# Single-pass masks and forget sums, and pages of values laid over 64 partitions, in a two-group decoder step

## The chip, the cores and the metric

The kernel runs on one core of one Trainium2 chip. The metric is the device time of one execution in microseconds (us); lower is better. Before the change three runs took 2627.09, 2624.44 and 2619.4 us, median 2624.44.

## The reference

One layer of a hybrid decoder trunk is computed for a prompt of 512 tokens and for a sample group of 8 sequences with 4 new tokens each, on the same weights (model width 2048, all in float32). A normalised input is projected into four mixers of 512 channels: causal pooling, a gated linear recurrence, forgetting attention (8 heads of 64) and stick-breaking attention (8 heads of 64). Their outputs are normalised by group, projected back and added; then a squared-ReLU MLP of width 8192 is added. The change touches only the two attentions:

```
# forgetting attention: c_all is the running sum of the log forget gates
s = q.k * 64**-0.5 + cq - ck_t;  s = where(kpos <= qpos, s, -inf)
p = softmax(s);  y = p @ v
# stick-breaking attention, strictly causal
z = q.k * 64**-0.5;  log_1m = where(kpos < qpos, log_sigmoid(-z), 0)
w = where(kpos < qpos, exp(log_sigmoid(z) + reverse_cumsum(log_1m) - log_1m), 0);  y = w @ v
```

The sample group attends to 2048 past tokens per sequence. They lie in 16 pages of 128 tokens, found through a page table; the keys of a page are 256 KB and its values are 256 KB, for each of the two attentions.

## The kernel before, in words

The kernel has three stages, closed off by `end_stage`. Stage 1 is the input projection with the pooling, the recurrence and the head norms. Stage 2 is both attentions. Stage 3 is the output projection and the MLP. In stages 1 and 3 TensorE multiplies in the type float32r: weights and activations are split into a high and a low part, `w_hi` and `w_lo`, and the products at L419 and L424 run on those.

Stage 2 is written out by hand as a loop of 32 units (`UNITS`, L1808 on TensorE, L1483 on VectorE). A unit i is one prompt head and one block of 128 queries, i = 4h + q, and it does that block for the forgetting head (x = 0) and the stick-breaking head (x = 1) together; its scores have n = 128(q+1) columns, so 128, 256, 384 and 512 in turn. Beside every two units one sample step u (0 to 15) runs: u = 2b + x is sequence b, attention x. So an even u (fox) runs beside units of 128 and 256 columns, an odd u (sb) beside 384 and 512. "Block" below means this period of one u and two units.

What a block does on TensorE, in order: `seq_scores(u)` (the queries against 2048 past keys, L1745, after all four `k_loaded` semaphores), `seq_combine(u-1)`, then for each unit a part of the early output projection (`early_product`, L1803), `scores(i)`, the transposes of the unit before (`turn`, L1703), and its product with the values (`weigh`, L1718). At the end of the second unit comes `seq_weigh(u)` (L1782): the transposed probabilities against the past values, four steps c = 0 to 3, each after its semaphore `v_loaded[c]` and each with 4 column strips j.

`scores(i)` (L1677) makes three kinds of product into PSUM: the forget sum (L1684: a one-hot column of the identity, repeated over 128 columns, picks the head's row of `c_prompt`, 8 rows by n columns), the query-key products (L1689), and one 128-column product per attention with the identity that adds the causal mask (L1692). All are float32. Ahead of L1689 TensorE waits for `s_diff` of the unit before (VectorE, L1405).

Loads: SyncE loads the keys (`load_keys`, L610, 16 DMAs per u into `k_ring`, 128 partitions by 2048 bytes a page). It has one buffer and waits at L621 for `d_score`, the end of `seq_scores(u)`, before it issues the keys of u+1; behind those keys on its queue come the stores of partial sums, the next early weights and the next residual halves. GpSimd loads the values (`load_values`, L812): 16 DMAs per u, page 4j + c into `v_ring` slot c, strip j, 128 partitions by 2048 bytes, one token per partition. It waits at L820 for `d_av`, so slot c is refilled when step c of the `seq_weigh` before is done. The sample probabilities `d_p` (128 rows by 512 keys, and 32 new ones) are transposed in four 128-column pieces in `seq_turn` (L1754).

At the start of stage 2 VectorE makes `c_prompt` with one scan (L1360), GpSimd clears the padded queries `q_pad` (L808), ScalarE stores ten transposed value tiles (`v_store`, L968), and TensorE waits for all of them and for the constants `dconst` (L1669 to L1675) before block 0.

Of the kernel before, what the change touches and what calls it, by code (L numbers as in the profile page):

```python
# [24 lines left out]
P = 128  # L25
# [16 lines left out]
ROWS = 32  # L42
# [18 lines left out]
V_SLOTS, X_SLOTS = 4, 6  # L61
# [5 lines left out]
for _name, _n in _W:  # L67
# [5 lines left out]
_K = [("ident", P), ("ones", P), ("same_head", P), ("fox_mask", P), ("sb_mask", P),  # L73
      ("pool_rec", GT * POOL_MAX), ("before", P), ("minus_one", 1)]
# [16 lines left out]
def build_step(nc, xT, weights, w_early, params, consts, dconsts, pool_w, lru_w, state_pool,  # L91
# [38 lines left out]
    decay = r.take("decay", [P, 2, PAGE * 4 + NEW])  # L130
    r = Region(A_RAW, A_PROJ)
# [49 lines left out]
    c_prompt = r.take("c_prompt", [HEADS, SEQ])  # L181
    xh = [r.take(f"xh{i}", [P, HALF]) for i in range(X_SLOTS)]
    r = Region(A_ACT, A_END)
    v_ring = r.take("v_ring", [P, V_SLOTS, 4, D_GROUP])
# [121 lines left out]
    new_lf = sem("new_lf")  # L306
    c_ready = sem("c_ready")
# [39 lines left out]
    v_loaded = [sem(f"v_loaded{c}") for c in range(4)]  # L347
# [396 lines left out]
    def _(pool):  # L744
# [61 lines left out]

        for x in range(2):
            own.then(nc.gpsimd.memset(q_pad[x][:], 0.0))  # L808
# [23 lines left out]
    def _(act):  # L832
# [89 lines left out]
        for c in range(C_OUT):  # L922
            g, step = lru_step(c)
            if c + 1 < C_OUT:
                high_part(act, c + 1)
            if c == 0:
                input_squares()
            if c == 1:
                softplus_lam()
            if c == 2:  # L930
                forget_log()
            if step == 1:
# [43 lines left out]
        for n in range(10):  # L976
            v_store(n)
        act.wait_ge(kv_stored, 16 * 3)
# [154 lines left out]
    def _(dve):  # L1133
# [179 lines left out]
        for c in range(C_OUT):  # L1313
# [38 lines left out]
            if c >= 1:  # L1352
# [7 lines left out]
        v.tensor_tensor_scan(c_prompt[:], ones[0:HEADS, 0:1].to_broadcast([HEADS, SEQ]), logit[:, 0:SEQ], 0.0,  # L1360
                             ALU.mult, ALU.subtract).then_inc(c_ready, 1)
# [3 lines left out]
        for x in range(2):  # L1365
# [6 lines left out]
            v.tensor_copy(k_new[x][:], proj[:, (FK, SK)[x], :, SEQ:]).then_inc(q_padded, 1)  # L1372

# [216 lines left out]
    def _(pe):  # L1590
# [78 lines left out]
        pe.wait_ge(signs_in, 16)  # L1669
        pe.wait_ge(v_stored, 10)  # L1670
# [6 lines left out]
        def scores(i):  # L1677
# [6 lines left out]
            mm(s[0], ident[0:HEADS, h:h + 1].to_broadcast([HEADS, P]), c_prompt[:, 0:n], start=True, stop=False)  # L1684
# [64 lines left out]
        def seq_turn(u):  # L1749
# [3 lines left out]
            for c in range(4):  # L1753
                nc.tensor.transpose(bank[:, 5, P * c:P * c + P], d_p[:, P * c:P * c + P], ident)  # L1754
# [19 lines left out]
        def seq_weigh(u):  # L1774
            x = u % 2
            pe.wait_ge(d_ptsb, u + 1)
            for c in range(4):
                pe.wait_ge(v_loaded[c], 64 * (u + 1))
                if c == 3:
                    mm(bank[3 * ROWS:, 6], pt_new[:, 3 * ROWS:], v_new[x][:], start=False, stop=False)  # L1780
                for j in range(4):
                    ins = mm(bank[ROWS * j:ROWS * j + ROWS, 6], pt_t[:, c, ROWS * j:ROWS * j + ROWS], v_ring[:, (4 * u + c) % V_SLOTS, j],  # L1782
# [92 lines left out]
def constants():  # L1875
# [10 lines left out]
    put("fox_mask", np.where(j <= i, 0, MASKED).astype(np.float32))  # L1886
    put("sb_mask", np.where(j < i, 0, MASKED).astype(np.float32))
    _, g, t = np.indices((P, GT, POOL_MAX))
    put("pool_rec", (1.0 / np.minimum(2 ** (g + 1), t + 1)).astype(np.float32).reshape(P, -1))
    put("minus_one", np.full((P, 1), -1, np.float32))  # L1890
# [130 lines left out]
```

## Time and profile before

| | |
|---|---|
| three runs, us | 2627.09, 2624.44, 2619.4 (median 2624.44) |
| the profiled execution's own time, us | 2623.07 |
| its span, first to last instruction, us | 2621.4 |
| TensorE busy, us (share) | 2534.5 (97%) |
| weight loads / VectorE / ScalarE / GpSimd | 89% / 51% / 35% / 8% |
| mean granted TensorE clock | 0.989 of full |
| HBM read / written, MB | 340.20 / 13.74 |

All times in the trace are us from the start of the span, unless marked ns. PE is the TensorE matmul, PEld its weight load, DVE is VectorE, ACT ScalarE, POOL GpSimd, SP SyncE. One float32 product shows as two records, one float32r product as one. Lines such as L1745 are lines of the kernel. "DMA share" is the mean busy share of the core's 16 DMA engines; packets of different queues can overlap, so short windows go a little over 1.

### The profile page before, as it was taken

Reading aid. Unit: us, or ns where it says so; the run is one execution under the profiler, and the core shown is the slowest. Engines: PE = TensorE matmul, PEld = TensorE weight load, DVE = VectorE, ACT = ScalarE, POOL = GpSimd, SP = SyncE. Lnnn points to the kernel's source line nnn. Section 1 sums busy time; section 2 is a strip of 40 time slices with the busy share of each in tenths; the row PEclk is TensorE's granted clock in tenths of the full one; section 3 lists DMA queues with packets and bytes.
Section 4 is the critical chain, followed back from the end, with each engine's and each line's share of the span. In section 5 each row is a group of like instructions: output and inputs, shape, how many; then the busy total and the mean of one; then the engine's idle time right before and its main releaser. Section 6 shows DMA issues by size and latency. Waiting matters only on the chain.

```text
span 2621.4 us, 43516 instructions
## 1 busy us (share of the span) xinstructions
PE 2534.5 (97%) x16842; PEld 2331.3 (89%) x16842; DVE 1325.9 (51%) x1860; ACT 914.9 (35%) x1577; POOL 204.2 (8%) x320
## 2 busy tenths in 40 slices
PE   7999999999999979999999999999999999999998
PEld 7999998755565559999999999999999999999998
DVE  6345455334343456454554554554554554554555
ACT  5244455423232344332332332332332332332333
POOL 2060000133333300000000000000000000000000
PEclk9999999999999979999999999999999999999999
DMA  6293232699999932222222222222222222222222
GB/s 205 85 67 106 95 98 82 249 335 369 355 367 361 331 151 88 90 83 95 81 85 93 81 91 87 81 86 92 81 91 87 81 85 93 81 91 87 89 89 101
DMA packets 115362, 356.75 MB, mean 136 GB/s; under 512 B 30937, under 2 KB 39130, under 8 KB 90978
## 3 DMA queue, kind: packets, MB, share of 16 engines
q1 hardware_dynamic: 94402, 286.34, 33.1%
q0 software_dynamic: 20768, 67.65, 7.1%
q8 instruction: 145, 2.38, 0.4%
q14 instruction: 47, 0.39, 0.0%
HBM read 340.20 MB, written 13.74 MB: 135 GB/s over the span
## 4 chain that ended last, share of the span: by engine, by line
PE 85%; DVE 5%; issue 3%; ACT 3%; DMA 2%; SPq 2%; ACTq 0%; DVEq 0%
PE bank L419 48%; PE bank L424 24%; PE bank L1803 3%; PE bank L1745 2%; PE bank L1782 2%; DMA w_raw<-weights 1%; ACT w_hi L406 1%; DVE sum_tmp L488 1%; PE bank L1689 1%; PE bank L1684 1%; SPq L618 1%; SPq L622 1%; PE bank L1605 1%; ACT sum_tmp L482 1%; PE bank L1718 1%
## 5 line engine op out<-in xcount | busy, mean ns | idle before, releaser
L419 PE MATMUL bank<-x_act,w_hi 128*128 128x364 f32 (+1 forms) x4848 | 1061.9, 329 | 25.4 <-DVE x_act L500 13.1
L419 PEld LDWEIGHTS bank<-x_act,w_hi 128*128 128x128 f32 x4848 | 774.0, 189 | 28.0 <-issue 13.6
L419 PE MATMUL bank<-hid,w_hi 128*128 128x364 f32 (+1 forms) x3456 | 728.8, 329 | 18.6 <-DVE sum_tmp L488 17.6
L424 PE MATMUL bank<-x_act,w_lo 128*128 128x272 f32 x3232 | 650.5, 287 | 1.4 <-issue 1.4
L488 DVE TENSOR_TENSOR sum_tmp<-sum_tmp,bank 128x544 f32<-128x544 f32 x336 | 241.9, 720 | 723.2 <-ACT sum_tmp L482 723.2
L419 PEld LDWEIGHTS bank<-hid,w_hi 128*128 128x128 f32 x3456 | 555.0, 188 | 28.7 <-DVE sum_tmp L488 25.9
L424 PEld LDWEIGHTS bank<-x_act,w_lo 128*128 128x128 f32 x3232 | 563.1, 189 | 3.5 <-issue 2.2
L481 ACT ACTIVATE sum_tmp<-bank 128x184 f32<-128x184 f32 x336 | 108.7, 323 | 1021.9 <-PE bank L419 1021.8
L424 PE MATMUL bank<-hid,w_lo 128*128 128x272 f32 x2304 | 429.1, 287 | 0.0
L410 DVE TENSOR_TENSOR w_lo<-w_raw,w_hi 128x2048 fp32r<-128x2048 f32 x173 | 396.9, 2294 | 52.1 <-ACT w_hi L406 46.9
L424 PEld LDWEIGHTS bank<-hid,w_lo 128*128 128x128 f32 x2304 | 379.1, 188 | 0.0
L406 ACT ACTIVATE w_hi<-w_raw 128x2048 fp32r<-128x2048 f32 x173 | 331.4, 1916 | 8.8 <-DMA w_raw<-weights 8.8
L1524 DVE TENSOR_TENSOR x_res<-x_res,sum_tmp 128x544 f32<-128x544 f32 x272 | 196.8, 724 | 7.1
L482 ACT ACTIVATE sum_tmp<-bank 128x360 f32<-128x360 f32 x336 | 156.6, 466 | 0.0
L1803 PE MATMUL bank<-proj,wo 128*128 128x272 f32 x512 | 137.1, 399 | 3.3 <-DVE xh L1481 3.3
L488 DVE TENSOR_TENSOR proj<-proj,bank 128x544 f32<-128x544 f32 x36 | 25.9, 720 | 166.9 <-ACT proj L482 166.9
L1803 PEld LDWEIGHTS bank<-proj,wo 128*128 128x128 f32 x512 | 89.2, 190 | 20.1 <-issue 7.4
L821 POOL DMA_DIRECT2D v_ring<-sb_v x128 | 68.9, 538 | 142.7 <-issue 81.9
L821 POOL DMA_DIRECT2D v_ring<-fox_v x128 | 68.9, 539 | 135.8 <-issue 79.4
L481 ACT ACTIVATE proj<-bank 128x184 f32<-128x184 f32 x36 | 11.6, 323 | 173.9 <-PE bank L419 173.9
L1380 DVE TENSOR_REDUCE stat<-bank 128x1 f32<-128x128 f32 (+3 forms) x32 | 15.7, 492 | 110.8 <-PE bank L1692 110.8
L836 ACT ACTIVATE pa<-bank 128x128 f32<-128x128 f32 (+3 forms) x32 | 14.0, 438 | 150.8 <-PE bank L1692 150.8
(225 smaller groups left out, 1555.1 us busy)
## 6 DMA issues: line engine op xcount, KB each, us to landing
w_raw<-weights SPq DMA_DIRECT2D x173, 1024.0 KB, 4.8
k_ring<-fox_k SPq DMA_DIRECT2D x128, 256.0 KB, 5.1
v_ring<-fox_v POOLq DMA_DIRECT2D x128, 256.0 KB, 5.1
k_ring<-sb_k SPq DMA_DIRECT2D x128, 256.0 KB, 5.2
v_ring<-sb_v POOLq DMA_DIRECT2D x128, 256.0 KB, 5.4
wo<-w_early SPq DMA_DIRECT2D x16, 512.0 KB, 6.3
x_in<-xT SPq DMA_DIRECT2D x4, 1088.0 KB, 10.8
kv_out<-proj SPq DMA_DIRECT2D x4, 1088.0 KB, 9.8
```

What stands on the lines that cost most here:

```text
L406: nc.scalar.activation(w_hi[c0 % 2][:], w_raw[c0 % 2][:], ACT.Copy).then_inc(w_high, 1)
L410: nc.vector.tensor_tensor(w_lo[c0 % 2][:], w_raw[c0 % 2][:], w_hi[c0 % 2][:].bitcast(F32), ALU.subtract).then_inc(w_low, 1)
L419: ins = nc.tensor.matmul(bank[:, base + b, 0:n], hi, row[:, t:t + n], start=begin, stop=end)
L424: ins = nc.tensor.matmul(bank[:, base + b, 0:HALF], lo, row[:, t:t + HALF], start=False, stop=False)
L481: nc.scalar.activation(out[:, :, 0:EXTRA], bank[0:rows, b:b + 2, HALF:SPAN], ACT.Copy)
L482: nc.scalar.activation(out[:, :, EXTRA:], halves(bank[0:rows, b + 2, 0:2 * THIRD]), ACT.Copy).then_inc(extra, 1)
L488: nc.vector.tensor_tensor(out, out, bank[0:rows, b:b + 2, 0:HALF], ALU.add).then_inc(evac, 1)
L821: pool.dma_start(v_ring[:, n % V_SLOTS, j], (fox_v, sb_v)[x][bass.ds(page, 1)].rearrange("a p n -> (a p) n")).then_inc(v_loaded[c], 16)
L1524: v.tensor_tensor(x_res[:, t], x_res[:, t], sum_tmp[n % 2][:], ALU.add).then_inc(added, 1)
L1745: ins = mm(bank[ROWS * j:ROWS * j + ROWS, 4], q_pad[x][:, b, a], k_ring[:, j, :, a], start=(x == 1 and a == 0), stop=(a == 3))
L1782: ins = mm(bank[ROWS * j:ROWS * j + ROWS, 6], pt_t[:, c, ROWS * j:ROWS * j + ROWS], v_ring[:, (4 * u + c) % V_SLOTS, j], start=(c == 0), s ...
L1803: ins = mm(bank[:, 7, 0:HALF], wo[t % 2][:, k], y, start=(k == 0), stop=(k == 2 * GT - 1))
```

## The change

Four edits, all for stage 2:

- The masks: the two 128-column masks become one constant `diagonal` of 129 columns, and it and the identity are rounded copies of type float32r (three small ScalarE copies in stage 1, beside chunk 4). L1692 multiplies in float32r.
- The forget sums: the scan writes `pc`, ScalarE copies its float32r rounding into rows 0 to 7 of `c_prompt`, VectorE writes the rest into rows 64 to 71, GpSimd clears the tensor first, and L1684 becomes one float32r product over 72 rows with a constant that has a one in both rows of a head.
- The values: a page lies in 64 partitions of 4096 bytes (two tokens per partition); page c goes to partitions 0 to 63 for even c and 64 to 127 for odd c. There are two semaphores instead of four, and GpSimd waits once per two slots.
- The transposes at L1754 take every second column of two pages' 256 keys, so that rows and values match; the products at L1782 take `v_ring[:, c // 2, j, c % 2]`.

```diff
@@ load_values, GpSimd
-                n = 4 * u + c
+                m, o = c // 2, HEAD_DIM * (c % 2)
                 for j in range(4):
...
-                    if j == 0 and n >= V_SLOTS:
-                        pool.wait_ge(d_av, n - V_SLOTS + 1)
-                    pool.dma_start(v_ring[:, n % V_SLOTS, j],
-                                   (fox_v, sb_v)[x][bass.ds(page, 1)].rearrange("a p n -> (a p) n")
-                                   ).then_inc(v_loaded[c], 16)
+                    if j == 0 and c % 2 == 0 and u >= 1:
+                        pool.wait_ge(d_av, 4 * u - 2 + 2 * m)
+                    pool.dma_start(v_ring[o:o + HEAD_DIM, m, j].rearrange("p t n -> p (t n)"),
+                                   (fox_v, sb_v)[x][bass.ds(page, 1)].rearrange("a (p t) n -> (a p) (t n)", t=2)
+                                   ).then_inc(v_loaded[m], 16)
@@ GpSimd, start of stage 2
+        nc.gpsimd.memset(c_prompt[:].bitcast(F32), 0.0).then_inc(c_cleared, 1)
@@ ScalarE, stage 1, beside chunk 4
+                f(ident_r[:], ident, ACT.Copy)
+                f(diagonal_r[:], cc("diagonal", 0, P + 1), ACT.Copy)
+                f(two_rows_r[:], cc("two_rows", 0, HEADS), ACT.Copy).then_inc(const_round, 1)
@@ ScalarE, start of stage 2, after the fifth v_store
+                f(c_prompt[0:HEADS], pc[0:HEADS], ACT.Copy).then_inc(c_high, 1)
@@ VectorE, start of stage 2
-        v.tensor_tensor_scan(c_prompt[:], ...
+        v.tensor_tensor_scan(pc[0:HEADS], ...
...
+        v.tensor_tensor(c_prompt[HEAD_DIM:], pc[0:HEADS], c_prompt[0:HEADS].bitcast(F32), ALU.subtract).then_inc(c_ready, 1)
@@ scores, TensorE
-            mm(s[0], ident[0:HEADS, h:h + 1].to_broadcast([HEADS, P]), c_prompt[:, 0:n], start=True, stop=False)
+            mm(s[0], two_rows_r[0:HEAD_DIM + HEADS, h:h + 1].to_broadcast([HEAD_DIM + HEADS, P]), c_prompt[:, 0:n],
+               start=True, stop=False)
...
-                mm(s[x][:, P * q:n], ident, cc(("fox_mask", "sb_mask")[x], 0, P), start=False, stop=True
+                mm(s[x][:, P * q:n], ident_r[:], diagonal_r[:, x:x + P], start=False, stop=True
@@ seq_turn, TensorE
-                nc.tensor.transpose(bank[:, 5, P * c:P * c + P], d_p[:, P * c:P * c + P], ident)
+                keys = d_p[:, 2 * P * (c // 2):2 * P * (c // 2) + 2 * P].rearrange("p (k t) -> p t k", t=2)
+                nc.tensor.transpose(bank[:, 5, P * c:P * c + P], keys[:, c % 2], ident)
@@ seq_weigh, TensorE
-                pe.wait_ge(v_loaded[c], 64 * (u + 1))
+                if c % 2 == 0:
+                    pe.wait_ge(v_loaded[c // 2], 128 * (u + 1))
...
-                    ins = mm(..., v_ring[:, (4 * u + c) % V_SLOTS, j],
+                    ins = mm(..., v_ring[:, c // 2, j, c % 2],
```

## Rows read from the trace of the kernel before

**Rows 1.** Stage 2 by stretch: us, busy by engine, PEclk, DMA share, GB/s
```profile
503.00:926.00 423.00, 414.89 (x2828) 233.90 (x2825) 174.20 (x454) 132.25 (x374) 135.58 (x252) 1.00 0.96 347
```

**Rows 2.** Chain that ended last, stage 2: start us, us, what
```profile
528.54 5.34 PE bank L1745 x32
...
820.34 3.44 PE bank L1745 x29
...
845.15 3.44 PE bank L1745 x29
...
872.62 3.45 PE bank L1745 x29
```

**Rows 3.** Waits of TensorE, 530 to 925 us: waiter, releaser, us, times, longest
```profile
PE bank L1803 <- DVE xh L1481: 2.7, 8, 0.3
PE bank L1745 <- DMA k_ring<-sb_k: 1.2, 2, 0.7
```

**Rows 4.** Last two stick-breaking key loads of a block: duration ns, start; landing us
```profile
L622 SPq DMA_DIRECT2D k_ring<-sb_k x2: 337/338/338, 839.4 to 840.5; - x2
...
DMA to landing us min/median/max: 3.5/3.8/4.1
```

**Rows 5.** The same, last two forgetting key loads of the next block
```profile
L622 SPq DMA_DIRECT2D k_ring<-fox_k x2: 338/338/338, 864.2 to 865.3; - x2
...
DMA to landing us min/median/max: 4.7/5.0/5.3
```

**Rows 6.** Timeline of SyncE: the 16 key loads of one block
```profile
848.76 16.84 SPq L622 DMA_DIRECT2D k_ring<-fox_k  x16
```

**Rows 7.** Timeline of GpSimd, last value load of a block; landings of L821, 840 to 900
```profile
861.56 0.54 POOL L821 DMA_DIRECT2D v_ring<-sb_v  x1 [0.61 <-issue]
...
DMA to landing us min/median/max: 3.6/5.3/6.3
```

**Rows 8.** Timeline of TensorE, 845 to 898 us: start, us, what
```profile
850.52 0.91 PE L1684 MATMUL bank<-c_prompt,const 8*128 8x384 f32 x2
851.36 0.92 PE L1689 MATMUL bank<-proj 64*128 64x384 f32 x4
...
858.11 1.12 PE L1684 MATMUL bank<-c_prompt,const 8*128 8x512 f32 x2
859.16 1.13 PE L1689 MATMUL bank<-proj 64*128 64x512 f32 x4
860.22 0.71 PE L1692 MATMUL bank<-const 128*128 128x128 f32 x4
860.77 0.28 PE L1763 MATMUL bank<-d_r,dconst 128*128 128x1 f32 x2
...
865.82 2.78 PE L1782 MATMUL bank<-v_ring,pt_t 128*32 128x512 f32 x24
```

**Rows 9.** Timeline of VectorE: the instruction that gives s_diff in that block
```profile
858.38 0.56 DVE L1405 TENSOR_TENSOR pa<-bank,pc 128x384 f32<-128x384 f32 x1
```

**Rows 10.** Chain in stage 1: float32r high products of two successive k
```profile
447.25 0.49 PE bank L419 x3
448.00 0.50 PE bank L419 x3
```

**Rows 11.** DMA queues, 503 to 924 us: packets, MB, share of 16 engines
```profile
q1 hardware_dynamic: 45661, 79.05, 51.5%
q0 software_dynamic: 20438, 66.95, 44.0%
```

**Rows 12.** The fastest long stretch of the DMA engines, columns as in rows 1
```profile
865.00:874.00 9.00, 9.00 (x79) 3.43 (x82) 2.52 (x7) 0.90 (x2) 3.23 (x6) 1.00 1.05 409
```

**Rows 13.** Weight loads of the transposes at L1754, whole stage: ns min/median/max
```profile
L1754 PEld LDWEIGHTS bank<-const,d_p x64: 138/141/225, 516.0 to 914.1; 128*128 128x128 f32 x64
```

**Rows 14.** Timeline of ScalarE, its last store before block 0
```profile
500.48 0.57 ACT L836 ACTIVATE v_new<-bank 32x512 f32<-32x512 f32 x1
```

**Rows 15.** Timeline of TensorE, the first product of block 0
```profile
501.15 0.33 PE L1733 MATMUL bank<-dconst,const 128*96 128x32 f32 x2 [0.85 <-DMA dconst<-dconsts]
```

More of the change, by code:

```diff
@@ L58 @@
 Y_POOL, Y_LRU, Y_SB, Y_FOX = U_POOL, X_LRU, SQ, FQ
-V_SLOTS, X_SLOTS = 4, 6
+X_SLOTS = 6
 _W = [("norm1", 16), ("norm2", 16), ("out_g", 16), ("pool_scale", 4), ("conv_w", 16), ("conv_b", 4),
@@ L70 @@
 N_PARAM = _at
-_K = [("ident", P), ("ones", P), ("same_head", P), ("fox_mask", P), ("sb_mask", P),
-      ("pool_rec", GT * POOL_MAX), ("before", P), ("minus_one", 1)]
+_K = [("ident", P), ("ones", P), ("same_head", P), ("diagonal", P + 1),
+      ("two_rows", HEADS), ("pool_rec", GT * POOL_MAX), ("before", P), ("minus_one", 1)]
 CONST, _at = {}, 0
@@ L130, in build_step @@
     decay = r.take("decay", [P, 2, PAGE * 4 + NEW])
+    ident_r = r.take("ident_r", [P, P], F32R)
+    diagonal_r = r.take("diagonal_r", [P, P + 1], F32R)
+    two_rows_r = r.take("two_rows_r", [P, HEADS], F32R)
     r = Region(A_RAW, A_PROJ)
@@ L180, in build_step @@
     pc = r.take("pc", [P, SEQ])
-    c_prompt = r.take("c_prompt", [HEADS, SEQ])
+    c_prompt = r.take("c_prompt", [HEAD_DIM + HEADS, SEQ], F32R)
     xh = [r.take(f"xh{i}", [P, HALF]) for i in range(X_SLOTS)]
     r = Region(A_ACT, A_END)
-    v_ring = r.take("v_ring", [P, V_SLOTS, 4, D_GROUP])
+    v_ring = r.take("v_ring", [P, 2, 4, 2, D_GROUP])
     v_tok = [r.take(f"v_tok{x}", [P, GT, D_GROUP]) for x in range(2)]
@@ L306, in build_step @@
     new_lf = sem("new_lf")
+    const_round = sem("const_round")
+    c_cleared = sem("c_cleared")
+    c_sum = sem("c_sum")
+    c_high = sem("c_high")
     c_ready = sem("c_ready")
@@ L346, in build_step @@
     k_loaded = [sem(f"k_loaded{j}") for j in range(4)]
-    v_loaded = [sem(f"v_loaded{c}") for c in range(4)]
+    v_loaded = [sem(f"v_loaded{m}") for m in range(2)]
     d_score = sem("d_score")
@@ L931, in _ @@
                 forget_log()
+            if c == 4:
+                act.wait_ge(consts_in, 16)
+                f(ident_r[:], ident, ACT.Copy)
+                f(diagonal_r[:], cc("diagonal", 0, P + 1), ACT.Copy)
+                f(two_rows_r[:], cc("two_rows", 0, HEADS), ACT.Copy).then_inc(const_round, 1)
             if step == 1:
@@ L977, in _ @@
             v_store(n)
+            if n == 4:
+                act.wait_ge(c_cleared, 1)
+                act.wait_ge(c_sum, 1)
+                f(c_prompt[0:HEADS], pc[0:HEADS], ACT.Copy).then_inc(c_high, 1)
         act.wait_ge(kv_stored, 16 * 3)
@@ L1359, in _ @@
         dve.wait_ge(new_lf, 1)
-        v.tensor_tensor_scan(c_prompt[:], ones[0:HEADS, 0:1].to_broadcast([HEADS, SEQ]), logit[:, 0:SEQ], 0.0,
-                             ALU.mult, ALU.subtract).then_inc(c_ready, 1)
+        v.tensor_tensor_scan(pc[0:HEADS], ones[0:HEADS, 0:1].to_broadcast([HEADS, SEQ]), logit[:, 0:SEQ], 0.0,
+                             ALU.mult, ALU.subtract).then_inc(c_sum, 1)
         dve.wait_ge(head_norm, 8)
@@ L1372, in _ @@
             v.tensor_copy(k_new[x][:], proj[:, (FK, SK)[x], :, SEQ:]).then_inc(q_padded, 1)
+        dve.wait_ge(c_sum, 1)
+        dve.wait_ge(c_high, 1)
+        v.tensor_tensor(c_prompt[HEAD_DIM:], pc[0:HEADS], c_prompt[0:HEADS].bitcast(F32), ALU.subtract).then_inc(c_ready, 1)
         dve.wait_ge(kv_stored, 16 * 3)
@@ L1669, in _ @@
         pe.wait_ge(signs_in, 16)
+        pe.wait_ge(const_round, 1)
         pe.wait_ge(v_stored, 10)
@@ L1781, in seq_weigh @@
                 for j in range(4):
-                    ins = mm(bank[ROWS * j:ROWS * j + ROWS, 6], pt_t[:, c, ROWS * j:ROWS * j + ROWS], v_ring[:, (4 * u + c) % V_SLOTS, j],
+                    ins = mm(bank[ROWS * j:ROWS * j + ROWS, 6], pt_t[:, c, ROWS * j:ROWS * j + ROWS], v_ring[:, c // 2, j, c % 2],
                              start=(c == 0), stop=(c == 3))
@@ L1885, in constants @@
     put("same_head", (i // HEAD_DIM == j // HEAD_DIM).astype(np.float32))
-    put("fox_mask", np.where(j <= i, 0, MASKED).astype(np.float32))
-    put("sb_mask", np.where(j < i, 0, MASKED).astype(np.float32))
+    row, key = np.indices((P, P + 1))
+    put("diagonal", np.where(key <= row, 0, MASKED).astype(np.float32))
     _, g, t = np.indices((P, GT, POOL_MAX))
     put("pool_rec", (1.0 / np.minimum(2 ** (g + 1), t + 1)).astype(np.float32).reshape(P, -1))
+    row, h = np.indices((P, HEADS))
+    put("two_rows", (row % HEAD_DIM == h).astype(np.float32))
     put("minus_one", np.full((P, 1), -1, np.float32))
```

## The prediction

> **What bounds the kernel now.** I read the page first: TensorE is near full in stages 1 and 3, the DMA engines only in stage 2, and all edits but three small copies lie there. Then stage 2 by stretch [rows 1]: TensorE is busy 414.9 of 423 us at full clock, and the DMA engines 96% at 347 GB/s. Two resources are full at once, so a gain on one is worth only what the other lets through. The reader is to see both numbers in that one row.
>
> The chain of waits gives the period. From one fox score product to the next is 872.62 - 820.34 = 52.28 us for two blocks, fox to sb 24.81 and sb to fox 27.47 [rows 2]; 26.14 a block, 16 blocks. TensorE hardly waits in it: 2.7 us in 8 pieces for VectorE and 1.2 us in 2 for keys [rows 3].
>
> How near are the loads? The last sb key load is issued at 840.5 and lands about 3.8 us later, at 844.3, and its product starts at 845.15: slack 0.85 us [rows 2, 4]. The last fox key load is issued at 865.3 and lands about 5.0 later, 870.3, against 872.62: slack 2.3 [rows 2, 5]. The keys are a chain of their own, since they are issued only after the score product before: 16.8 us of issue, 4 to 5 of landing, 3.4 of product, 24 to 25.5 us a block [rows 2, 4 to 6]. The last value load is issued at 861.56 and lands by 866.9; `seq_weigh` starts at 865.82 and needs it for its last step, some 2.7 us on [rows 7, 8].
>
> The DMA engines themselves need 95.5% of 421 us, 402 us, or 25.1 us a block: 11.6 for the values (44.0%) and 13.5 for the rest (51.5%) [rows 11]. The block has 26.14. So the cover is one microsecond.
>
> **Part 1: single passes.** Start to start, a forget sum of 512 columns takes 859.16 - 858.11 = 1.05 us and one of 384 takes 0.84 [rows 8]: 0.21 per 128 columns and 0.21 beside, so 0.63 and 0.42 for 256 and 128. The two masks of a unit take 860.77 - 860.22 = 0.55. Float32r: 1632 columns and two weight loads take 0.75 us [rows 10], 0.06 per 128 columns. Taking 0.09 for the one weight load left (under half of the 0.21), the sums cost 0.33, 0.27, 0.21, 0.15, and two masks 0.22. Saved in two blocks: 0.72 + 0.57 + 0.42 + 0.27 + 4 x 0.33 = 3.3 us, 26 us in all. The other end: every float32r product in the trace has 272 columns or more. If the narrower ones gain nothing, 0.72 + 0.57 is left, 10 us in all. I take 26, since cost goes by columns at every width shown in float32.
>
> What of it reaches the end: `s_diff` comes at 858.38 + 0.56 = 858.94, and the query-key product behind the 512-column sum starts at 859.16 [rows 8, 9]. So only 0.2 of that 0.72 is free, and VectorE is late next: 2.8 per two blocks. The fox-to-sb part saves 1.35 but the sb keys have 0.85 of slack; the sb-to-fox part keeps its 1.45, within 2.3. Together 2.3 per two blocks, 18 us. The DMA floor of 25.1 allows (26.14 - 25.1) x 16 = 17 us at best. I take 14 as what part 1 gives if the values load as now.
>
> **Part 2: the start.** ScalarE's new copy stands before its last five stores, the last of which ends at 501.05, while TensorE's first product starts at 501.15 [rows 14, 15]. A copy of 8 by 512 costs like the one of 32 by 512, 0.57: +0.5 us, once. The clearing (GpSimd, ahead of the padded queries and the value loads), the subtraction on VectorE and the three copies in stage 1 have more room than that: TensorE stands behind ScalarE there, and in stage 1 ScalarE is half idle. Uncovered they would be 0.5 us each.
>
> **Part 3: strided transposes.** 64 weight loads of 141 ns now step over every second element [rows 13]. Between nothing and twice as long: 0 to 9 us. I take 0, as a weight load overlaps the product before it.
>
> **Part 4: the coarser wait.** The refill of a slot pair starts one step of `seq_weigh` later, 2.7/3 = 0.9 us, and step 2 now needs both pages: at 865.82 + 1.8 = 867.6 against the landing at 866.9 + 0.9 = 867.8 [rows 7, 8]. 0 to 0.9 us a block, 0 to 14 us in all; alone I take 0.2 a block, 3 us, and in the forecast it is inside the DMA wait.
>
> **Part 5: pages in 64 partitions.** First what it cannot give. The value queue moved 66.95 MB in 20438 packets [rows 11]. Rows of 2048 bytes sent one by one would be 32,700 packets; about 250 loads with 64 packets each, and 16 small ones each for the completion, are 20,000. So the values already travel 4096 bytes a packet, and the number of packets does not fall. GpSimd may write each load's list faster than 0.54 us, but it is not what anyone waits for.
>
> Then what it can cost. No load in this trace lands in half of the partitions, so its rate has to be bounded. Lower end: as now, 25.1 us of DMA a block. Upper end: if each value packet takes twice as long, because 16 engines write into half of the memory's width, 25.1 + 11.6 = 36.7 us. Between them, by bytes: full speed is 409 GB/s [rows 12]. The values of a block, 4.19 MB, at half of it take 20.5 us; the rest, 79.05/16 = 4.94 MB, takes 12.1. One after the other that is 32.6; if the half of the rest that goes to the free partitions passes beside the values it is 26.5. The middle is 29.6. Four loads in a row go to the same half and are issued 1.15 us apart (228 GB/s), so the two halves do not relieve each other within one queue. A gain is excluded by the packet count.
>
> With the DMA floor above 26.14, TensorE's savings are worth nothing and the keys come late. A wait has a second price: after the one long wait for keys, the score product took 5.34 us instead of 3.44 [rows 2]. I add 0.8 a block, between nothing and that 1.9. The block is 30.4, so +4.3 x 16 = +68 us; with +0.5, the profiled 2623.07 becomes 2691.6. That run is 1.4 under the median of 2624.44. I predict 2691 us.
>
> The Trainium skill, SBUF — State Buffer, section "Door 1: The DMA port swizzle", states this as a rule: partitions 0 to 63 reach only 8 of 16 ports, and a 1 MiB load there ran at 196 GB/s against 328 over all 128. It also says that two loads to the two halves gained 6% only. By its ratio, 409 x 0.6 = 245 GB/s, the values would take 17.1 us (an estimate from that page) and the block 23.2 to 29.2 before any wait. No run here shows the rule yet; it speaks for the forecast's side.
>
> **Rivals.**
> *A. Faster: the layout is neutral.* TensorE and keys set the block; it falls to 25.3. Mechanism and place: the masks and sums in `scores`, 14 us off, 0.5 on: 2609 us (2601 to 2616). For it: packets keep their 4096 bytes, and the queues drain at 409 GB/s when pressed [rows 12]. Against it: a share of 96%. It holds as long as value loads lengthen by less than 1 us a block.
> The Trainium skill, Perfetto Trace Analysis, section "DMA Optimizations", goes further: going from 2 KB to 4 KB can improve throughput greatly. By it the DMA floor would fall and up to 26 us would show, 2598. The packet count speaks against it for these loads.
> *B. No change.* Narrow float32r products gain nothing (10 us instead of 26), the doubled transposes, or step 2's wait at 0.2 to 0.5 a block, eat the rest: 10 - 0.5 - 3 to 8 leaves 0 to 6: about 2621. This is also the case in which the edit doesn't do what it says.
>
> **How the numbers follow.** Forecast 0.52, A 0.40, B 0.08. The forecast's own range is 2630 (block at 26.5) to 2775; I cut its tail at 2755. About 0.05 lies under 2604 and 0.1 over 2755, so the range is 2604 to 2755. A change under 0.3%, 8 us, is not told from none; of A nearly all lies beyond it, of B nothing. Faster 0.40, same 0.08, slower 0.52. The forecast leads because the DMA engines are full, and the layout has only a loss to offer them; it leads by little because the loss's size stands in no row.
>
> **What would show it.** Right: value loads land later than 5.3 us, TensorE waits at L1745 for `k_ring` and at L1782 for `v_ring` in most blocks, the queue q0 has as many packets as now but takes more than 11.6 us a block, blocks are near 30 us, the granted clock of stage 2 falls under 1.00. Part 1 right: L1684 under 0.35 us and L1692 near 0.22 a unit, with TensorE's busy time down by some 20 us. Wrong: a DMA share of q0 as before and a block of 25 to 25.5 us (A); records of L1692 no shorter (B).

## The result, and the profile after

The changed kernel takes 2872.54 us (median of four runs, 2854.91 to 2877.1) against 2625.14 us for the kernel before (2619.4 to 2627.09): ratio 1.0945, 95% interval 1.0922 to 1.0967. The prediction had 2691 us and a range up to 2755. The profiled execution took 2875.01 us, with a span of 2873.3 and a granted clock of 0.939. Its lines lie lower in the file: L1769 is the product against the past keys (before L1745), L1809 the one against the past values (L1782), L1713 query-key, L1707 forget sum, L1716 masks, L629 and L830 the loads of keys and values, L576 the norm sums that end stage 2 (L569).

First by stage. In both kernels the middle stage runs from the first product against past keys to the first norm sum, and the last stage from the second norm sum, 12.85 us later, to the end of the span. Timeline of TensorE, kernel before, then after:

```profile
502.96 0.63 PE L1745 MATMUL bank<-k_ring,q_pad 128*32 128x512 f32 x3
...
935.32 2.15 PE L569 MATMUL bank<-n_tmp,const 128*128 128x272 f32 x4 [4.22 <-DVE n_tmp L537]
948.17 2.18 PE L569 MATMUL bank<-n_tmp,const 128*128 128x272 f32 x4 [10.71 <-DVE n_tmp L537]
```
```profile
501.68 0.63 PE L1769 MATMUL bank<-k_ring,q_pad 128*32 128x512 f32 x3
...
1169.19 2.15 PE L576 MATMUL bank<-n_tmp,const 128*128 128x272 f32 x4 [4.21 <-DVE n_tmp L544]
1182.04 2.18 PE L576 MATMUL bank<-n_tmp,const 128*128 128x272 f32 x4 [10.70 <-DVE n_tmp L544]
```

The middle stage grew from 432.4 to 667.5 us, +235; the last from 1673.2 to 1691.3, +18, though nothing in it was edited; the start shrank by 1.3. That is the whole +252 of the two spans. All later stage lengths are taken in the same way.

The middle stage in one row, and two windows of 10 us in it, columns as in [rows 1]:

```profile
503.00:1165.00 662.00, 433.82 (x2736) 230.03 (x2728) 174.78 (x456) 132.84 (x375) 128.06 (x251) 0.79 0.87 221
...
700.00:710.00 10.00, 0.00 (x0) 0.00 (x0) 0.00 (x0) 0.00 (x0) 3.57 (x7) 0.50 1.05 261
...
719.00:729.00 10.00, 9.30 (x49) 3.67 (x49) 0.00 (x0) 2.00 (x4) 0.00 (x0) 0.67 0.25 71
```

The DMA engines are still busy 87% of a stage half as long again, but move 221 GB/s and not 347. TensorE idles 228 us. The granted clock, averaged over the whole stage with its idle time, is 0.79: it stands at 0.50, the lower of the two levels, where TensorE waits (700 to 710 us), and the first products behind such a wait still run at that level. What it waits for, 530 to 1160 us (against [rows 3]):

```profile
PE bank L1769 <- DMA k_ring<-sb_k: 154.8, 8, 21.0
PE bank L1809 <- DMA v_ring<-fox_v: 54.7, 7, 9.3
PE bank L1713 <- DVE pa L1426: 4.6, 8, 0.6
```

The two key kinds now differ, as the chain shows (against [rows 2], cut as marked): every other block, from fox to sb, waits.

```profile
582.34 3.45 PE bank L1769 x29
...
604.75 30.41 DMA k_ring<-sb_k
635.30 6.11 PE bank L1769 x32
...
654.93 1.84 PE bank L1830 x8
...
657.58 2.71 PE bank L1809 x24
...
664.31 3.45 PE bank L1769 x29
```

So 582.34 to 635.30 is 53.0 us (before 24.81), 635.30 to 664.31 is 29.0 (27.47), and the product behind the wait takes 6.11 in place of some 3.6 (3.45 is for 29 of its 32 records). The queues, 503 to 1165 us (against [rows 11]), and the loads by kind over the whole span (KB each, median us from issue to landing), kernel before, then after:

```profile
q1 hardware_dynamic: 45517, 78.92, 44.9%
q0 software_dynamic: 20374, 66.76, 42.0%
```
```profile
k_ring<-fox_k SPq DMA_DIRECT2D x128, 256.0 KB, 5.1
v_ring<-fox_v POOLq DMA_DIRECT2D x128, 256.0 KB, 5.1
k_ring<-sb_k SPq DMA_DIRECT2D x128, 256.0 KB, 5.2
v_ring<-sb_v POOLq DMA_DIRECT2D x128, 256.0 KB, 5.4
```
```profile
k_ring<-fox_k SPq DMA_DIRECT2D x128, 256.0 KB, 2.9
v_ring<-fox_v POOLq DMA_DIRECT2D x128, 256.0 KB, 9.7
k_ring<-sb_k SPq DMA_DIRECT2D x128, 256.0 KB, 21.1
v_ring<-sb_v POOLq DMA_DIRECT2D x128, 256.0 KB, 9.9
```

Shares times stretch give the time of 16 engines. Values: 0.420 x 662 = 278 us, before 0.440 x 421 = 185: +93. The rest, keys mostly: 297 against 217, +80, though no key load was edited. Engines idle or with other queues: 87 against 19, +68. The three make +241 for a stretch 241 us longer.

Only the sb keys are late; the fox keys land sooner than before. The issues of two blocks tell why: SyncE's keys with their landings, and the first value load of the next pair on GpSimd.

```profile
667.92 24.53 SPq L629 DMA_DIRECT2D k_ring<-sb_k  x16
...
726.48 17.23 SPq L629 DMA_DIRECT2D k_ring<-fox_k  x16
```
```profile
DMA to landing us min/median/max: 9.2/22.4/30.3
```
```profile
DMA to landing us min/median/max: 2.5/3.0/3.6
```
```profile
744.96 0.51 POOL L830 DMA_DIRECT2D v_ring<-fox_v  x1 [37.48 <-PE bank L1809]
```

GpSimd issues all 32 value loads of the pair between 660 and 707 us, beside the sb keys, and none in the 37 us after that, while the fox keys load. Each later pair shows the same order. So value loads into half of the partitions and the sb keys hold each other up, and the time in which the DMA engines have little to do comes right behind (share 0.25 from 719 to 729 us, above), because the next keys wait for the late score product and the next values for `seq_weigh`.

### The profile page after: what moved, and what is told of

It reads as the page before. It is cut to its first block, busy times and chain, and to the rows that moved or that the text cites. A ratio compares the mean times of both kernels' runs of the same rounds, so it can differ in the third digit from the quotient of the medians.

```text
span 2873.3 us, 43332 instructions
## 1 busy us (share of the span) xinstructions
PE 2561.8 (89%) x16746; PEld 2335.0 (81%) x16746; DVE 1326.1 (46%) x1861; ACT 915.9 (32%) x1581; POOL 197.8 (7%) x321
## 3 DMA queue, kind: packets, MB, share of 16 engines
q0 software_dynamic: 20768, 67.65, 9.8%
## 4 chain that ended last, share of the span: by engine, by line
PE 74%; DMA 10%; DVE 5%; SPq 5%; issue 4%; ACT 3%; ACTq 0%; DVEq 0%
PE bank L426 44%; PE bank L431 22%; DMA k_ring<-sb_k 8%; SPq L629 3%; PE bank L1769 3%; SPq L625 2%; ACT w_hi L413 1%; DMA w_raw<-weights 1%; PE bank L1830 1%; PE bank L1809 1%; DVE sum_tmp L495 1%; PE bank L1626 1%; PE bank L1713 1%; ACT sum_tmp L489 1%; DVE w_lo L417 0%
## 5 line engine op out<-in xcount | busy, mean ns | idle before, releaser
L1769 PE MATMUL bank<-k_ring,q_pad 128*32 128x512 f32 x512 | 75.6, 737 | 154.8 <-DMA k_ring<-sb_k 154.8
L1769 PEld LDWEIGHTS bank<-k_ring,q_pad 128*32 128x32 f32 x512 | 23.4, 131 | 193.1 <-issue 193.1
L1809 PE MATMUL bank<-v_ring,pt_t 128*32 128x512 f32 x512 | 77.1, 714 | 62.4 <-DMA v_ring<-fox_v 62.4
```

The lines of the kernel that those rows point to most:

```text
L1769: ins = mm(bank[ROWS * j:ROWS * j + ROWS, 4], q_pad[x][:, b, a], k_ring[:, j, :, a], start=(x == 1 and a == 0), stop=(a == 3))
```

## The experiments

Each changes what its diff shows, with cuts marked. "Passes" is the new masks and forget sums with the old value layout. A ratio is to the kernel before, timed beside it; its own median lay between 2621 and 2631 us. Stage lengths come from one trace each. Where two kernels have the same middle stage they differ by up to 5 us (440.0, 436.5 and 439.1 in e1, g1 and p1; 423.0 and 418.1 in g2 and g4), so less than that is not resolved.

**e1_passes: the single passes alone** (every edit of the layout undone in the changed kernel)
```diff
-                    pool.dma_start(v_ring[o:o + HEAD_DIM, m, j].rearrange("p t n -> p (t n)"),
-                                   (fox_v, sb_v)[x][bass.ds(page, 1)].rearrange("a (p t) n -> (a p) (t n)", t=2)
+                    pool.dma_start(v_ring[:, n % V_SLOTS, j],
+                                   (fox_v, sb_v)[x][bass.ds(page, 1)].rearrange("a p n -> (a p) n")
```


> Only the single passes are kept: values again one token per partition over 128 partitions, four semaphores, plain transposes. Theory H (all of the loss comes from loads that land in one half of the partitions): value packets back at 11.6 us of DMA a block, block 25.0 to 25.6 us, time 2605 to 2613 us, faster than before by 0.5%. Rival S (part of the loss comes from the single passes or their set-up, through a clock that falls when TensorE has less to do): time 2625 us or above, granted clock of stage 2 under 0.98.

2640.02 us, ratio 1.007 (1.0057 to 1.0083): slower by 0.7%. Theory H, and the prediction's 14 us for part 1, fail; rival S holds in its numbers (2625 us or above, clock of the stage under 0.98). Middle stage 440.0 (+7.6), last stage 1688.3 (+15.0). By stretch, middle and last stage:

```profile
503.00:937.00 434.00, 399.74 (x2725) 225.62 (x2717) 175.14 (x456) 133.18 (x377) 134.08 (x250) 0.97 0.93 335
955.00:2641.00 1686.00, 1642.95 (x10886) 1628.84 (x10884) 895.85 (x1060) 539.80 (x911) 0.00 (x0) 0.99 0.26 88
```

TensorE has 15 us less to do in the middle stage (399.7 against 414.9) but idles 34 us in place of 8. Its waits, 530 to 930 us, and two score products behind a wait:

```profile
PE bank L1769 <- DMA k_ring<-sb_k: 17.3, 7, 3.3
```
```profile
583.52 5.34 PE L1769 MATMUL bank<-k_ring,q_pad 128*32 128x512 f32 x32 [2.96 <-DMA k_ring<-sb_k]
...
691.56 3.64 PE L1769 MATMUL bank<-k_ring,q_pad 128*32 128x512 f32 x32 [1.73 <-DMA k_ring<-sb_k]
```

After a wait of 2.96 us the product takes 5.34, after one of 1.73 it takes 3.64: the longer pause is followed by products at the lower clock (granted clock 0.50 from 586 to 588 us), for 1.7 us more. What the passes save turns into waits, and the waits cost on top. The last stage differs in another way, in pauses that wait for nothing (955 us to the end; the kernel before has no such line):

```profile
PE bank L426 <- issue: 7.0, 6, 1.6
```

These pauses are 7.0 of the 15 us. About as much again lies behind them: in windows of 10 us the granted clock is under 1.00 more often than in the kernel before (0.98 and 0.68 in the two windows from 1490 us, for one), which adds up to some 12 us of clock lost against 3 (an estimate from those windows).

**e2_layout: the layout alone** (old masks and sums, new value loads, transposes and waits; against the changed kernel)
```diff
-            mm(s[0], two_rows_r[0:HEAD_DIM + HEADS, h:h + 1].to_broadcast([HEAD_DIM + HEADS, P]), c_prompt[:, 0:n],
-               start=True, stop=False)
+            mm(s[0], ident[0:HEADS, h:h + 1].to_broadcast([HEADS, P]), c_prompt[:, 0:n], start=True, stop=False)
...
-                mm(s[x][:, P * q:n], ident_r[:], diagonal_r[:, x:x + P], start=False, stop=True
+                mm(s[x][:, P * q:n], ident, cc(("fox_mask", "sb_mask")[x], 0, P), start=False, stop=True
```


> Only the layout is kept: float32 masks and forget sums as before, pages in 64 partitions. Theory H: the loss is whole, 2870 to 2885 us, since TensorE waits for loads and 26 us more of its work are hidden in the waits. Rival S (the two edits add up): 2850 us or less for this one alone, the rest from the passes.

2860.36 us, ratio 1.0911 (1.0885 to 1.0937). Middle stage 675.5, last stage 1673.3. The time lies between the two forecasts (2870 to 2885, and 2850 or less), but the stages are clear: the layout carries the whole loss of the middle stage and nothing of the last.

**e3_alternate: changed kernel, loads in turn to lower and upper half**
```diff
-            for c in range(4):
-                m, o = c // 2, HEAD_DIM * (c % 2)
-                for j in range(4):
+            for m in range(2):
+                for k in range(8):
+                    j, c = k // 2, 2 * m + k % 2
+                    o = HEAD_DIM * (c % 2)
```


> The changed kernel with its value loads issued in turn to the lower and the upper half, instead of four to one half and four to the other. Theory H with queues that keep step (each of the 16 engines does its share of one load before the next): a load still fills one half alone, packets stay near 264 ns, time within 1% of 2872 us. If the engines' queues drift apart by a load, both halves are written at once: value packets at 200 ns or less and 2700 us or less. Rival F (the 4096-byte rows or the 64 rows are the cost, not where they land): no difference at all.

2858.18 us, 1.0903; middle stage 656.8, 11 less than the changed kernel. Theory H's 1% holds (2858.18 against 2872.54); the order of the halves is not the cause.

**e4_every_second: the same rows of 4096 bytes, in every second partition** (the probabilities keep the changed kernel's order, so the sample attentions pair them with other tokens; the amount of work is the same)
```diff
-                    pool.dma_start(v_ring[o:o + HEAD_DIM, m, j].rearrange("p t n -> p (t n)"),
+                    pool.dma_start(v_ring[c % 2:P:2, m, j].rearrange("p t n -> p (t n)"),
```


> The changed kernel with a page in every second partition (even pages in partitions 0, 2, 4 to 126, odd pages in 1, 3 to 127): the same 64 rows of 4096 bytes, the same packets, but over both halves. The transposed probabilities are not reordered to match, so the sample attentions pair them with other tokens. Theory H: value packets back near 159 ns, block 25 to 25.6 us, 2603 to 2615 us. Rival F (64 rows or 4096-byte rows are slow wherever they land): 2850 to 2890 us.

2638.75 us, 1.0058 (1.0045 to 1.0072); middle stage 434.1. Its loads, whole span:

```profile
v_ring<-fox_v POOLq DMA_DIRECT2D x128, 256.0 KB, 5.2
k_ring<-sb_k SPq DMA_DIRECT2D x128, 256.0 KB, 5.6
v_ring<-sb_v POOLq DMA_DIRECT2D x128, 256.0 KB, 5.0
```

Its values are as fast as before. One slice decides: 64 partitions spread over all 128 cost nothing, the lower or the upper 64 cost 230 us. Whether 64 adjacent partitions across the middle, 32 to 95, are slow too was not tried. The time is over theory H's 2603 to 2615 by what the passes lose in e1_passes, and beside that kernel (2638.75 against 2640.02) rows of 4096 bytes gain nothing that the times resolve.

**e5_rows_2048: adjacent 64 partitions, but two rows of 2048 bytes in each**
```diff
-                    pool.dma_start(v_ring[o:o + HEAD_DIM, m, j].rearrange("p t n -> p (t n)"),
-                                   (fox_v, sb_v)[x][bass.ds(page, 1)].rearrange("a (p t) n -> (a p) (t n)", t=2)
+                    pool.dma_start(v_ring[o:o + HEAD_DIM, m, :, j],
+                                   (fox_v, sb_v)[x][bass.ds(page, 1)].rearrange("a (p t) n -> (a p) t n", t=2)
```


> The changed kernel with its pages still in 64 partitions, but the two tokens of a partition 8192 bytes apart, so each row sent is 2048 bytes. Theory H (where the rows land sets the rate): value packets near 264 ns as in the changed kernel, 2855 to 2880 us. Rival F (rows of 4096 bytes are what is slow): packets back to 159 ns, 2660 us or less.

2863.91 us (one run), as theory H has it; middle stage 651.9. The length of a row is not the cause either. It doesn't set the packets: GpSimd's queue has 20768 of them over the whole run here, as in the kernel before, the changed kernel and e4.

**e7_values_alone_half and e8_values_alone_full: changed layout and old layout, keys loaded for the first block only** (the later blocks compute with those; 15 x 4.19 = 62.9 MB of key loads are left out, not the 3.75 MB of the expectation)
```diff
-                load_keys(u + 1)
+                sp.wait_ge(d_score, u + 1)
...
-                pe.wait_ge(k_loaded[j], 64 * (u + 1))
+                pe.wait_ge(k_loaded[j], 64)
```


> The changed kernel, but the keys are loaded for the first block only; the later fifteen blocks compute with that first block's keys, so their 3.75 MB of key loads are left out and the result is another. The value loads stay as changed, each page in 64 partitions. It measures what the value loads in the new layout take when no keys share the queues. Theory H (half of the partitions halves the rate at which values land; 264 us for 22 of GpSimd's waits and keys queued behind them come from that): value packets still take about 260 ns, and a block in which values come from memory takes 33 to 45 us without any key wait; the middle stage takes 520 to 620 us. Rival K (the values are only slow because they and the keys meet in the same engines): without keys the value packets fall under 200 ns, and the middle stage takes 410 to 440 us.

> The kernel with the single passes alone, values in 128 partitions as in the kernel before, and again keys for the first block only, the same loads left out. Theory H: value packets at about 160 ns, and the middle stage at 405 to 425 us with no key waits at all (440 with them); the difference to the kernel ahead of it in the list is the price of the half-partition layout by itself. Rival (the middle stage is bound by value loads in the old layout as well): it stays at 435 to 440 us.

One run each: 2657.73 and 2613.67 us. Middle stages 456.5 and 405.4. The value queue, 503 to 940 us, first half, then full:

```profile
q0 software_dynamic: 20139, 66.04, 66.3%
```
```profile
q0 software_dynamic: 20453, 67.01, 48.5%
```

While the engines work for it, the queue moves 66.04 / (0.663 x 437 us) = 228 GB/s into halves and 67.01 / (0.485 x 437) = 316 into all partitions: 0.72. A value packet takes 0.663 x 437 x 16 / 20139 = 0.230 us, against 0.166 in e8 and 0.218 in the changed kernel by the same working: under theory H's 260 ns, but not under the 200 of theory K. So the slower rate is there without keys; the stage, though, lies between the two forecasts. By itself the layout costs 456.5 - 405.4 = 51 us. With keys it costs 667.5 - 440.0 = 227. The other 176 come only with the keys that share the engines. And in the full layout, with no keys to wait for, the blocks show what the passes are worth to TensorE; the score products of fox, sb and fox:

```profile
798.87 0.63 PE L1769 MATMUL bank<-k_ring,q_pad 128*32 128x512 f32 x3
...
822.29 0.63 PE L1769 MATMUL bank<-k_ring,q_pad 128*32 128x512 f32 x3
...
848.55 0.63 PE L1769 MATMUL bank<-k_ring,q_pad 128*32 128x512 f32 x3
```

23.42 and 26.26 against 24.81 and 27.47: 1.39 and 1.21 saved.

**p1_pad and p2_before_pad: where the last loop begins in TensorE's instructions.** The passes take 192 instructions out of TensorE's stream ahead of the last stage. p1 is e1_passes with 192 semaphore increments at the head of the stream, p2 the kernel before with 64.
```diff
+        for _ in range(192):      # p2: 64
+            pe.sem_inc(padding, 1)
```


> Single passes only, with 192 increments of an unused semaphore at the very start of TensorE's program, as many instructions as the single passes took out of it (96 products and 96 weight loads). Theory I (stage 3 got 15 us longer, 1688 against 1673 us, though its code is the same, because TensorE's loop begins at another place of the instruction stream and is fetched later at each turn): the six waits put down to issue at L426 vanish, stage 3 is back at 1673 to 1676 us and the whole at 2622 to 2627 us. Rival J (stage 3 is longer for what stage 2 left behind: clock, queues, layout in memory): stage 3 stays at 1688 and the whole at 2640 us.

> The kernel before with 64 increments of an unused semaphore at the start of TensorE's program. Theory I: its loop moves by 64 instructions; if the place matters, stage 3 (1673 us) may lengthen to 1688 with six to seven waits for issue; which places are bad is not known, so this maps one. Rival J: 1673 us and 2622 us whatever is added.

p1: 2649.15 us, 1.0066 (1.0044 to 1.0087); last stage back to 1673.2 as theory I has it, but not the time of 2622 to 2627, since the increments themselves put the middle stage's start off by 23 us. p2: 2646.45 us, 1.0062 (1.0041 to 1.0083); last stage 1690.7, with the pauses of e1_passes:

```profile
PE bank L420 <- issue: 6.7, 6, 1.7
```

An unchanged loop costs 15 to 18 us more or less by how many instructions stand before it. That count is not all of it: e7_values_alone_half, with as many TensorE instructions as the changed kernel, has a last stage of 1682.3 us against 1691.3 (one run), and why is open.

**f1_filler: e1_passes with two useless products ahead of the sb keys' wait**
```diff
+            if x == 1:
+                mm(bank[:, 4], ident, dc("own_head", 0, D_GROUP), start=True, stop=True)
+                mm(bank[:, 4, 0:2 * P], ident, dc("own_head", 0, 2 * P), start=True, stop=True)
```


> Single passes only, with two useless float32 products (512 and 256 columns, 1.5 us) ahead of the wait for the stick-breaking keys of every odd step, so that TensorE comes to it as late as before the change. Theory C (stage 2 got 7.6 us longer because TensorE, being early, waits long enough for its clock to fall to 1.2 GHz, and the score product then takes 5.3 us instead of 3.6): most of the eight waits fall under 1.5 us, fewer than 2 score products take 5.3 us, and stage 2 is 432 us or less, with 12 us more work in it. Rival D (the keys themselves land later and the wait is not what costs): stage 2 gets longer by the filler, 445 us or more.

2629.3 us, 0.9996 (0.9984 to 1.0008); middle stage 430.2 in place of 440.0 (436.5 in g1, below), with more work in it. Waits for keys from 480 us on are 8.6 us, none over 2.6, and one sb score product takes 5.3 us where e1_passes has five of 5.3 to 6.4: theory C. Work in place of idling keeps the clock up: that part of e1_passes' loss is the clock. Its last stage was 1678.2, which its added instructions, which shift the loop too, may explain; that was not tried.

**g1, g2, g4: both side effects taken away, step by step.** g1 puts 48 products (192 instructions) in front of the second norm sum's wait; g2 also reads the 16 page numbers of the next keys before SyncE's wait; g4 makes the 48 products one column wide.
```diff
@@ TensorE, ahead of the second norm sum: g1, g2; in g4 the last line in place of the one above it
+                for _ in range(48):
+                    mm(bank[:, 5, 0:1], ident, ones[:, 0:1], start=True, stop=True)
+                    mm(bank[0:1, 5, 0:1], ident[:, 0:1], ones[:, 0:1], start=True, stop=True)
@@ load_keys, SyncE: g2, g4, g3
+                pages16 = [sp.value_load(ids[0:1, PAGES * b + k:PAGES * b + k + 1], min_val=0,
+                                         max_val=POOL_PAGES - 1) for k in range(16)]
...
                         sp.wait_ge(d_score, u)
```


> The kernel with the single passes alone (its stage of score and value products took 440 us, its last stage 1688.3), and 48 products of one column, 192 TensorE instructions in all, put in front of the wait of the second norm sum, where TensorE idles about 10.7 us. Nothing else changes. Theory I (the last stage of the passes kernel is 15 us longer only because its TensorE loop begins 192 instructions earlier in the instruction stream): the last stage comes back to 1673 to 1675 us, its extra pauses of about 1.5 us per loop turn go, and the time is 2624 to 2628 against 2640. Rival (the last stage is longer because of what the passes themselves do, a lower clock carried over or another arrival of loads): last stage stays at 1686 to 1690 and the time at 2638 to 2642, or more by the added products.

> The kernel before this one in the list (single passes, loop placed by the 192 added instructions), and SyncE reads the sixteen page numbers of the next block before it waits for the scores of the running block, so that its 16 key loads are issued with less between them. Theory C (the passes alone bring nothing in the middle stage because the time saved turns into waits for keys of about 3 us, after which each score product costs 1.7 us more at a lower clock): keys that are requested 1 to 3 us earlier shorten these waits from 23 us in 8 to under 10, the blocks fall from 26.8 to 25 us and from 27.9 to 26.2, the middle stage takes 418 to 428 us, and the time is 2604 to 2614, faster than both kernels. Rival (the middle stage is bound by the bytes that the load queues carry, not by when they are asked for): the keys land as late as before, the middle stage stays at 436 to 441 us and the time at 2622 to 2628.

> Single passes, early page numbers for the keys, and the loop of the last stage put back to its place by 48 added products; but each added product has one column of weights in place of 128. The 48 wide ones took 20.48 us (0.43 us each), of which only the 10.7 us of a wait were free, so that the second norm sum began 22.3 us behind the first in place of 12.9. Theory (the time added was the loading of 128 columns of weights): the narrow ones take under 10.7 us, the second norm sum begins 12.9 to 14 us behind the first, the last stage stays at 1673 us, and the time is 2611 to 2615 against 2622, faster than the kernel before by 0.2 to 0.4%. Rival (a product in four passes costs 0.43 us however narrow its weights): the gap stays at 22 us and the time at 2620 to 2624.

g1: 2638.25 us, 1.006 (1.0047 to 1.0073). The last stage is 1673.2 as theory I has it; but the 48 products took 20.5 us where 10.7 were free:

```profile
941.71 20.48 PE L1870 MATMUL bank<-const 128*128 128x1 f32 x96
962.05 2.16 PE L576 MATMUL bank<-n_tmp,const 128*128 128x272 f32 x4
```

Those products run at the lower clock, which is 0.50 from 940 to 962 us, as it is there in the kernel before. g2: 2622.1 us, 1.0002 (0.9994 to 1.0011): middle stage 423.0 in place of 436.5, waits for sb keys 7.5 us in 5, both in theory C's range; the time of 2604 to 2614 does not come, with the same 20.5 us of products in it. g4 (timeline, and the middle stage by stretch):

```profile
930.00 2.54 PE L1874 MATMUL bank<-const 128*1 128x1 f32 x96
940.78 2.18 PE L576 MATMUL bank<-n_tmp,const 128*128 128x272 f32 x4 [8.24 <-DVE n_tmp L544]
```
```profile
503.00:920.00 417.00, 397.17 (x2765) 226.88 (x2762) 177.31 (x473) 136.26 (x383) 137.42 (x256) 0.99 0.97 357
```

The narrow products take 2.5 us. Middle stage 418.1, last stage 1673.1; 2618.29 us against 2630.52 for the kernel before, ratio 0.996 (0.9946 to 0.9973): the 0.4% of the theory, though not its 2611 to 2615 us. This version, single passes without the layout, beats both kernels.

**g3_before_keys: the kernel before, page numbers read early** (the SyncE edit of g2, on the kernel before)

> The kernel before the change, and only SyncE's order changed: it reads the sixteen page numbers of the next block before it waits for the scores of the running one. It tells how much of the gain of the version with single passes (middle stage 423.0 us against 436.5 of the same kernel without this) belongs to the single passes. Theory C (single passes are worth about 10 us once the keys come early enough, and earlier keys alone save only the 5 us or so that the kernel before spends in key waits and their aftermath): middle stage 426 to 432 us, time 2615 to 2621. Rival (the whole gain is the earlier keys, the passes give nothing): middle stage 419 to 424 us, time 2608 to 2613.

2627.45 us against 2630.52, 0.9984 (0.9972 to 0.9996), only 0.16% faster; middle stage 427.3, in theory C's range (its time of 2615 to 2621 is missed). The passes are the other 427.3 - 418.1 = 9.2 us, and the medians differ by as much, 2627.45 - 2618.29 = 9.2.

## Why the prediction was wrong

The direction and the mechanism were right: the DMA engines set the stage, the layout only takes. The size was wrong by 3.5 times (+68 us forecast in the middle stage, +235 measured), and the result lies outside the range. Step by step:

- *Part 5, lower and upper bound, is the step that failed.* The values came out inside its bounds: 278 us of engine time against 185, 1.5 times; "by bytes" gave 20.5 us a block, it is 17.4. But the bounds let only the value packets slow. The rest was priced at 12.1 to 13.5 us a block and took 297 / 16 = 18.6; and the sum treated the engines as always busy, while they idle 87 us. Its own upper end of 36.7 us a block stands for 2792 us (not the 2775 of its range) and is passed too: a block takes 667.5 / 16 = 41.7. Loads of keys can be issued only after the score product before, so a late key load is a pause for the DMA engines too: I had written that chain out in the first part, and did not put it beside the slower values. e7 and e8 separate the two: 51 us from the values' own rate, 176 from the keys with them. The rows of the result show that company decides: sb keys, issued beside the 32 value loads of a pair, land after some 21 us (5.2 before), fox keys, with none beside them, after 2.9 (5.1 before). Why the keys slow there, although half of their partitions are free of values, was not tried; that they meet the values in the same engines' queues is argued only.
- The Trainium skill, SBUF — State Buffer, "Door 1: The DMA port swizzle", gives 196 against 328 GB/s for a load into partitions 0 to 63, 0.60. The runs agree in kind: 228 against 316 GB/s, 0.72 (e7, e8), and e4_every_second shows that it is the half that costs, not the 64 partitions. The 6% that two loads to the two halves gained together stands in that page's section "Can I just issue two DMAs to hit both halves?". Sending them in turn down one queue (e3) gave a middle stage of 656.8 against 667.5 us, 1.6%: little as well.
- *The price behind a wait* (0.8 us a block, 1.6 for two) was near the right size for the score product: behind the sb waits it takes 4.9 to 6.6 us in place of 3.6, once in two blocks. (The 1.9 behind it sets 32 records, 5.34, against 29, 3.44; like with like it is 5.34 - 3.64 = 1.7.) What was far too small is the wait itself: 154.8 us in 8 for keys and 54.7 in 7 for values are some 27 us for every two blocks, where the forecast had 2 x (29.6 - 26.14) = 7.
- *Packet count* right: 20374 against 20438. *Blocks of 30.4 us each* wrong in form too: 53 and 29 in turn. Only sb keys wait, since no value loads are issued beside the fox keys.
- *Part 1* right in size at the place of action, by two errors that cancel. 1.39 and 1.21 us of a block pair (e8) against 1.35 and 1.45 forecast. In the first of the two, with the weight load ahead of it, a forget sum saves 0.35 and 0.51 us (forecast 0.27 and 0.42), and the masks of a unit save 0.27 (0.33). The signs named for it, L1684 under 0.35 us and L1692 near 0.22 a unit, did not come: the records below are longer, and two masks take 0.28 us from start to start in e8; `s_diff` is late next, as forecast (4.6 us in 8 at L1713). In the stage, masks and sums (means of overlapping records):

```profile
L1716 PE MATMUL bank<-diagonal_r,ident_r 128*128 128x128 f32 x64 | 14.0, 301 | 0.0
...
L1707 PE MATMUL bank<-c_prompt,two_rows_r 72*128 72x512 f32 x8 | 4.8, 595 | 0.0
L1707 PE MATMUL bank<-c_prompt,two_rows_r 72*128 72x128 f32 x8 | 3.4, 425 | 0.0
```

- *What of part 1 reaches the end*: 14 us forecast, a loss of 18 us measured (e1: 2640.02 against 2621.98). So rival A, held at 0.40, could not have come true even with a neutral layout. It failed by two terms. The working had the sb keys' slack of 0.85 us, and so a wait of 0.5 us in every second block, 4 us in all; e1 has 17.3 us in 7 waits, and the longer ones lower the clock, a price that the prediction set in part 5 and left out here. And, in no step at all, fewer instructions move the last loop. With the last loop put back and the keys asked for earlier the passes give 9.2 us (g4 against g3).
- *Part 2*: +0.5 us forecast, the start is 1.3 us shorter, and it varies from 500.1 to 511.1 us among kernels without p1's increments; not resolved. *Parts 3 and 4*, strided transposes and coarser waits: e4 has both, and its middle stage is not longer than that of e1 (434.1 against 440.0), so neither costs anything to be seen.
- *Rival B* didn't occur; the narrow float32r products do gain.

## What to carry to other kernels

Before a load is laid out anew, ask which partitions it touches: the lower or the upper 64 run at 0.7 of the rate (e7, e8) and slow the loads that are in flight beside them, while every second partition costs nothing. Where a transfer may start only when its consumer has run, slack is not one number per queue: slow one queue and the other's round trip grows, and both bounds must be added up with the pauses in. And after any edit that saves work under a nearly full DMA, look at what ends the waits and at the granted clock before calling the saving a saving.

## What the runs showed that I had not expected

- The place of a loop in TensorE's instruction stream is worth 15 to 18 us here: 192 instructions fewer or 64 more gives 1688 to 1691 us, 192 put back gives 1673. With it come six `issue` pauses of up to 1.7 us and a lower clock behind them. Which placements are good was not mapped, and e7's 1682.3 us shows that more than the place has a part.
- A TensorE semaphore increment is not free: 192 of them moved TensorE's first product from 13.0 to 30.5 us, at least 0.09 us each, and its first score product from 500.6 to 523.6. The 64 of p2 did not move the first product, which waits for VectorE until 13 us.
- A one-column float32 product costs 0.43 us with 128 columns of weights (20.48 / 48, g1) and 0.05 us with one (2.54 / 48, g4), both at a granted clock of 0.50: the columns of weights are nearly all of it.
- Useless work ahead of a wait can shorten a stage: from 440.0 us in e1_passes (436.5 in g1) to 430.2 in f1_filler.
